# Rows repeated over partitions: TensorE selections and ScalarE copies replaced by DMAs inside SBUF, in a decoder step with a mixture of experts

## The chip, the cores and the metric

The kernel runs on one core of one Trainium2 chip. The metric is the device time of one execution in microseconds (us), median of several runs. A profile shows one execution: busy times and waits of TensorE (PE; PEld is its weight load), VectorE (DVE), ScalarE (ACT), GpSimd (POOL) and SyncE (SP), and what the DMA engines moved. SP computes nothing here; its program is a list of DMA issues and of semaphore waits, taken strictly in order. All its transfers go through one hardware queue (q1 in the profile).

## The reference, cut to what matters

One layer for 256 prompt tokens (one sequence) and 64 sample tokens (8 sequences of 8). Width 1024, everything in float32.

```
mod = silu(c) @ w_ada + b_ada                 # c: one row per sequence, 9 in all
sh1, sc1, gt1, sh2, sc2, gt2 = split(mod, 6)  # 1024 columns each
h = rmsnorm(x, g_mix) * (1 + sc1) + sh1
merged = sigmoid(ga) * (attention(h) @ w_pa) + sigmoid(gb) * (retention(h) @ w_pb)
x = x + gt1 * (merged @ w_o)
h2 = rmsnorm(x, g_ffn) * (1 + sc2) + sh2
x = x + gt2 * moe(h2)                         # top 4 of 32 experts, SwiGLU, 12.6 MB of weights each
y = rmsnorm(x, g_final)
```

The change is about sh2 (the "shift rows") and gt2 (the "gate rows"). Each is 9 rows of 1024: one for the prompt, 8 for the sample sequences. The mixture of experts needs them with tokens on partitions, so the prompt's row must stand on all 128 partitions (sh2p, gt2p), and each sample sequence's row on 8 of 64 partitions (sh2s, gt2s).

## The kernel before, in words

Each engine has a program written out by hand, and semaphores tie them together (wait_ge on one engine, then_inc on another). There is no scheduler: the order in the file is the order on the engine.

**Before the experts.** Weights come in 2 MB tiles. Tiles 17 to 25 hold, among others, the eight tiles of the modulation (w_mid), which modulation_step multiplies on TensorE between the branch projections. DVE's modulation_out(i) (line 2275) copies the sums of half i out of PSUM into mod_rows[i]: in half 0 stand gt1 and sh2, in half 1 sc2 and gt2. Partitions 64 to 72 and 96 to 104 of mod_rows hold the 9 rows of sh2 (or gt2), 512 columns in each group, and a small DMA puts the matching piece of b_ada on partition 73 and 105. modulation_transposes (line 1498) makes the column forms gt1T, sh2T, a2T from the same tile.

**Spreading the rows.** spread_rows(i) on TensorE (line 1509) multiplies 32 partitions of mod_rows[i] by the constant selp (ones on row 0 and on row 9, the bias), which adds the bias and repeats the prompt's row over 128 partitions, and by sels for the sample rows. ACT copies the results out of PSUM: sh2p and sh2s at lines 861 to 864, gt2p and gt2s at 874 to 877. spread_rows(0) runs right ahead of the output projection, spread_rows(1) (in final_gate_rows) after its third column tile.

**The output projection** is out_tile(c), c = 0 to 7 (line 1551): tile 26 of the weights serves c = 0 to 3, tile 27 the rest. Between the column tiles stand shift_logits (line 1575, sh2 times the router's weights wr, waits on rw_here, that is on the load of wr), spread_shift_logits (1582) and the router's product (1559). After each column tile DVE's x1_tile makes the new x, ACT squares it (869) and POOL adds the squares (680). Then come the norm, the router's logits and the top 4 on DVE (line 2345 to 2356; 2356 writes the selection), the position count on PE (1635, 1637), and h2 = normed x + shift: prompt tile 0 by DVE (2360), prompt tile 1 scaled by ACT (886) and shifted by POOL (683), the samples by DVE (2514). x_rows (1680) gathers the first expert's rows.

**The experts.** Weights come as 2 MB chunks, 6 to an expert, into 8 slots. gate_up_bias (line 1745) opens an expert; for the first one it waits on late_here, which counts the load of bgu (b_gate_up, line 541). gate_up (1759) takes chunks 0 to 3, down (1786) chunks 4 and 5. Chunk n is issued by SP once chunk n - 8 is used, so from here on the stream of chunks is tied to PE's progress. The first eight chunks are issued as their slots come free, during the output projection.

**SP's list around the change:** modulation tiles 21 to 23, the bias rows of half 0, b_router, tile 24, tiles 26 and 27 (w_out), wr, the bias rows of half 1, chunks 0 to 3 of expert 0, b_down, the final norm's row, chunk 4, one chunk of expert 1, chunk 5, bgu, another chunk of expert 1.

Of the kernel before, what the change touches and what calls it, by code (L numbers as in the profile page):

```python
# [16 lines left out]
ALU = mybir.AluOpType  # L17
# [55 lines left out]
def constants():  # L73
# [16 lines left out]
    t["selp"] = np.tile(((r % 32 == 0) | (r % 32 == 9))[:, None], (1, P))  # L90
    t["sels"] = ((r % 32)[:, None] == 1 + np.arange(NS)[None, :] // DS) | (r % 32 == 9)[:, None]
# [73 lines left out]
def kern(nc, a):  # L165
    with ExitStack() as ctx:
# [77 lines left out]
        mod_rows = [xr[:, 512 * i:512 * i + 512] for i in range(2)]  # L244

# [34 lines left out]
        def rt(at, n):  # L280
# [72 lines left out]
        h2s_done, rstd2_done, gT_tr, gT_done, ainit_mm, g2_mm, g2_done, late_here, flag_done = (sem(n) for n in (  # L353
            "h2s_done", "rstd2_done", "gT_tr", "gT_done", "ainit_mm", "g2_mm", "g2_done", "late_here", "flag_done"))
# [7 lines left out]
        yf_done, mul_done = sem("yf_done"), sem("mul_done")  # L362
        col_done, wo_mm, ut_done, pool_sum = sem("col_done"), sem("wo_mm"), sem("ut_done"), sem("pool_sum")
# [38 lines left out]
        def _(sp):  # L402
# [100 lines left out]
            load_modulation(20, 2)  # L503
            sp.wait_ge(sa_tr, PAIRS)
# [14 lines left out]
            load_bias_rows(1, g_here)  # L519
# [16 lines left out]
            sp.wait_ge(g2_mm, 2)  # L536
# [52 lines left out]
        def _(pool):  # L589
# [91 lines left out]
            pool.wait_ge(part_done, 5)  # L681
            pool.wait_ge(rows_done, 13)
            nc.gpsimd.tensor_tensor(h2[:, 1, :], h2[:, 1, :], sh2p, ALU.add).then_inc(pool_sum, 1)

        @block.scalar
        def _(act):
# [173 lines left out]
            act.wait_ge(tb_mm, 3)  # L860
            nc.scalar.activation(sh2p, bank(0, 2), ACT.Copy).then_inc(part_done, 1)
            act.wait_ge(tb_mm, 4)
            nc.scalar.activation(sh2s[0:NS, 0:BANK], bank(4)[0:NS], ACT.Copy)
            nc.scalar.activation(sh2s[0:NS, BANK:D], bank(4)[NS:P], ACT.Copy).then_inc(part_done, 1)
# [6 lines left out]
            for c in range(3):  # L871
                x1_square(c)
            act.wait_ge(g2_mm, 1)
            nc.scalar.activation(gt2p, bank(0, 2), ACT.Copy).then_inc(g2_done, 1)
            act.wait_ge(g2_mm, 2)
            nc.scalar.activation(gt2s[0:NS, 0:BANK], bank(4)[0:NS], ACT.Copy)
            nc.scalar.activation(gt2s[0:NS, BANK:D], bank(4)[NS:P], ACT.Copy).then_inc(g2_done, 1)
            for c in range(3, KT):
                x1_square(c)
# [20 lines left out]

            x1_rows_out(0)
# [109 lines left out]
        def _(pe):  # L1011
# [489 lines left out]
            def spread_rows(i, signal):  # L1501

                for name in ("selp", "sels"):
                    if i == 0 and name == "sels":
                        pe.wait_ge(rows_done, 12)
                    for k in range(2):
                        rows = slice(64 + 32 * k, 96 + 32 * k)
                        out = bank(4)[NS * k:NS * k + NS, :] if name == "sels" else bank(k)
                        last = nc.tensor.matmul(out, const(name)[rows], mod_rows[i][rows], start=True, stop=True)
                    last.then_inc(signal, 1)  # L1510

# [51 lines left out]
            def router_rows():  # L1563

                pe.wait_ge(part_done, 7)
# [20 lines left out]
            def final_gate_rows():  # L1586
                pe.wait_ge(g_here, 64)
                pe.wait_ge(part_done, 6)
                spread_rows(1, g2_mm)

            for c in range(KT):
# [5 lines left out]
                if c == 2:  # L1597
                    final_gate_rows()
# [21 lines left out]
            pe.wait_ge(g2_done, 2)  # L1620
# [261 lines left out]
        def _(dve):  # L1882
# [401 lines left out]
            for i in range(2):  # L2284
# [12 lines left out]
                if i == 0:  # L2297
                    dve.wait_ge(tb_mm, 1)
                    for half, (dst, at) in enumerate(((gt1T, 2 * KT), (sh2T, 3 * KT))):
                        nc.vector.tensor_tensor(by_chunk(dst), columns_of(half), spread(badaT[:, at:at + KT]),  # L2300
                                                ALU.add).then_inc(col_done, 1)
# [330 lines left out]
```

## Time and profile before

| | |
|---|---|
| runs, median (lowest to highest) | 1392.13 us (1390.81 to 1394.26) |
| the profiled execution, device time | 1390.95 us |
| its span in the profile | 1389.1 us |
| PE busy | 1353.6 us (97% of the span) |
| DVE, ACT, POOL busy | 501.1, 219.8, 67.6 us |
| moved by DMA | 487.81 MB, mean 351 GB/s |
| chain that ended last | PE 76%, DMA 18%, DVE 3%, ACT 1% |

PE is busy nearly all the time, and from about 486 us on the DMA engines move 425 to 430 GB/s without a break, so both are at work all through the experts. The experts' first matmul of gate_up stands at 455.0 us.

### The profile page before, as it was taken

The page shows a single profiled execution, that of the slowest core. Times are in us where ns is not written, and L with a number is a line of the kernel's source. Part 1 is how long each engine was busy: PE and PEld are TensorE (multiplying, and loading weights), DVE is VectorE, ACT ScalarE, POOL GpSimd, SP SyncE. Part 2 cuts the span into 40 slices and gives each one's busy share as a digit, 9 for nine tenths or more (in the row PEclk, how much of TensorE's full clock was granted, in tenths as well). Part 3 has the DMA queues.
Part 4 walks back from the last instruction along what each step waited for, and adds up shares of the span by engine and source line. Part 5 has one row for each costly group of instructions (what it writes and reads, how often), then busy time and mean ns, then how long its engine had stood idle before and what let it go on. Part 6 is the DMA issues. An engine that isn't in the chain of part 4 may idle for free.

```text
span 1389.1 us, 17563 instructions
## 1 busy us (share of the span) xinstructions
PE 1353.6 (97%) x6742; PEld 549.9 (40%) x6742; DVE 501.1 (36%) x1081; ACT 219.8 (16%) x407; POOL 67.6 (5%) x65
## 2 busy tenths in 40 slices
PE   8999999999999999999999999999999999999996
PEld 4544555555456333333333333333333333333332
DVE  3245887853124322332233222422223222233225
ACT  2111232121022211111111111111111111111102
POOL 1003402220001000000000000000000000000000
PEclk9999999999999999999999999999999999999998
DMA  9424354387877799999999999999999999999994
GB/s 387 161 98 166 122 128 159 105 311 272 345 314 307 280 428 428 428 426 428 428 430 427 428 428 430 428 428 427 430 428 428 427 430 429 427 428 429 430 425 185
DMA packets 62302, 487.81 MB, mean 351 GB/s; under 512 B 8327, under 2 KB 30407, under 8 KB 33836
## 3 DMA queue, kind: packets, MB, share of 16 engines
q1 hardware_dynamic: 59948, 482.43, 84.4%
q0 software_dynamic: 1152, 4.19, 0.8%
q8 instruction: 30, 0.49, 0.1%
q10 hardware_dynamic: 1152, 0.52, 0.1%
q14 instruction: 20, 0.16, 0.0%
HBM read 483.01 MB, written 4.08 MB: 351 GB/s over the span
## 4 chain that ended last, share of the span: by engine, by line
PE 76%; DMA 18%; DVE 3%; ACT 1%; issue 0%; SPq 0%; DVEq 0%
PE ps L1759 23%; PE ps L1786 12%; DMA z<-in_w_gate_up 10%; DMA ring<-in_w_gate_up 7%; PE ps L1068 6%; PE ps L1069 5%; PE ps L1680 5%; PE ps L1083 3%; PE ps L1731 3%; PE ps L1551 3%; PE ps L1745 2%; PE ps L1046 2%; PE ps L1735 1%; PE ps L1393 1%; PE ps L1382 1%; DMA ring<-in_w_mid 1%
## 5 line engine op out<-in xcount | busy, mean ns | idle before, releaser
L1759 PE MATMUL ps<-ring,z 128*64 128x512 f32 x1552 | 343.7, 594 | 9.8 <-DMA ring<-in_w_gate_up 9.1
L2455 DVE TENSOR_SCALAR actT<-ps 128x512 f32<-128x512 f32 x32 | 22.1, 692 | 589.6 <-PE ps L1759 589.6
L1759 PEld LDWEIGHTS ps<-ring,z 128*64 128x64 f32 x1552 | 108.5, 137 | 239.4 <-issue 217.6
L1786 PE MATMUL ps<-ring,z 128*64 128x512 f32 x752 | 167.7, 594 | 0.0
L1068 PE MATMUL ps<-ring,actT 128*128 128x512 f32 (+1 forms) x200 | 102.4, 594 | 1.3 <-DVE actT L1941 1.1
L1069 PE MATMUL ps<-ring,actT 128*128 128x512 f32 (+1 forms) x200 | 100.3, 583 | 0.0
L1786 PEld LDWEIGHTS ps<-ring,z 128*64 128x64 f32 x752 | 52.5, 137 | 109.9 <-issue 109.1
L1680 PE MATMUL ps<-z,actT 128*64 128x512 f32 x384 | 89.1, 597 | 0.2 <-DVE actT L2371 0.2
L1731 PE MATMUL ps<-z,aT 128*128 128x512 f32 x120 | 62.0, 619 | 0.0
L1759 PE MATMUL ps<-z 128*64 128x512 f32 x256 | 57.9, 594 | 3.0 <-DMA z<-in_w_gate_up 3.0
L2400 DVE TENSOR_TENSOR xr<-xr,z 128x512 f32<-128x512 f32 (+1 forms) x75 | 59.8, 797 | 2.6
L939 ACT ACTIVATE actT<-actT 128x512 f32<-128x512 f32 x30 | 18.8, 627 | 237.7 <-DVE actT L2455 237.7
L1069 PEld LDWEIGHTS ps<-ring,actT 128*128 128x128 f32 x200 | 38.0, 190 | 46.0 <-issue 45.0
L2392 DVE TENSOR_TENSOR z<-ps,z 128x512 f32<-128x512 f32 x60 | 41.4, 689 | 37.7 <-PE ps L1731 37.5
L1759 PE MATMUL ps<-more_w,z 128*64 128x512 f32 x240 | 54.5, 596 | 0.0
L924 ACT ACTIVATE z<-ps 64x512 f32<-64x512 f32 x30 | 17.7, 589 | 231.7 <-PE ps L1786 231.7
L1068 PEld LDWEIGHTS ps<-ring,actT 128*128 128x128 f32 x200 | 35.7, 190 | 42.2 <-issue 41.3
L1084 PE MATMUL ps<-ring,actT 128*64 128x256 f32 (+1 forms) x200 | 45.8, 379 | 0.0
L1083 PE MATMUL ps<-ring,actT 128*64 128x256 f32 (+1 forms) x200 | 45.8, 378 | 0.0
L2036 DVE MAX8 st<-ring 64x8 f32<-64x1032 f32 (+2 forms) x48 | 45.0, 937 | 1.3
L1680 PEld LDWEIGHTS ps<-z,actT 128*64 128x64 f32 x384 | 26.6, 137 | 46.3 <-issue 44.9
L2037 DVE MATCH_REPLACE8 ring<-st,ring 64x1032 f32<-64x1032 f32 (+2 forms) x48 | 44.1, 920 | 0.0
(370 smaller groups left out, 1305.1 us busy)
## 6 DMA issues: line engine op xcount, KB each, us to landing
ring<-in_w_gate_up SPq DMA_DIRECT2D x97, 2048.0 KB, 27.1
ring<-in_w_down SPq DMA_DIRECT2D x47, 2048.0 KB, 29.7
z<-in_w_gate_up SPq DMA_DIRECT2D x16, 2048.0 KB, 27.6
more_w<-in_w_gate_up SPq DMA_DIRECT2D x15, 2048.0 KB, 26.4
ring<-in_w_in SPq DMA_DIRECT2D x11, 2048.0 KB, 7.6
more_w<-in_w_down SPq DMA_DIRECT2D x9, 2048.0 KB, 30.6
ring<-in_w_mid SPq DMA_DIRECT2D x8, 2048.0 KB, 9.3
z<-in_w_down SPq DMA_DIRECT2D x8, 2048.0 KB, 33.0
```

The lines of the kernel that those rows point to most:

```text
L1068: nc.tensor.matmul(bank(b)[:, 0:w], hT[:, k, 0:P], w_z(i, k), **se)
L1069: last = nc.tensor.matmul(bank(b + 1)[:, 0:w], hT[:, k, P:2 * P], w_z(i, k), **se)
L1083: nc.tensor.matmul(bank(b)[0:NS, 0:h], hT[:, k, 2 * P:NTOK], w_z(i, k)[:, 0:h], **se)
L1084: last = nc.tensor.matmul(bank(b)[NS:P, 0:h], hT[:, k, 2 * P:NTOK], w_z(i, k)[:, h:w], **se)
L1551: last = nc.tensor.matmul(bank(6 + c % 2)[:, 0:NTOK], w[:, k, c % 4 * P:(c % 4 + 1) * P], hT[:, k, :], start=k == 0, stop=k == KT - 1)
L1680: last = nc.tensor.matmul(bank(3)[64 * i:64 * i + 64, :], S[:, t, :], h2[:, t, i * BANK:(i + 1) * BANK], start=t == 0, stop=t == 2)
L1731: nc.tensor.matmul(bank(b), SgT[:, t * P:(t + 1) * P], y[:, half * BANK:(half + 1) * BANK], start=True, stop=True).then_inc(cmb_mm, 1)
L1759: done = nc.tensor.matmul(bank(q // 2)[64 * (q % 2):64 * (q % 2) + 64, :], lhs, homes[home][4 * (k % 2) + q], start=False, stop=k == 7)
L1786: done = nc.tensor.matmul(bank(2)[64 * q:64 * q + 64, :], lhs, homes[home][2 * (k % 4) + q], start=k == 0, stop=k == 7)
L2036: step(nc.vector.max(m8, v))
L2037: step(nc.vector.match_replace(v, m8, v, TAKEN))
L2400: last = nc.vector.tensor_tensor(acc[0:n, t, c], acc[0:n, t, c], tmp3[t][0:n, c], ALU.add)
```

## The change

It does five things.

1. modulation_out(i) adds the bias on DVE, from bias_rows[i]: b_ada repeated over 9 partitions by DMA (four DMAs, issued early), in a region that POOL zeroes first (a memset of 128x1024).
2. spread_rows leaves TensorE (16 matmul instructions in all) and ACT (six copies). In its place SP issues, for each of sh2 and gt2, four DMAs from SBUF to SBUF: for each half of the columns one whose source is one row on one partition, read 128 times, and one whose source is 8 rows on 8 partitions, each read 8 times. That is 2 x 262,144 + 2 x 131,072 = 786,432 bytes written for each of the two.
3. Waits follow: DVE and POOL wait for sh2_here where they waited for ACT's copy; the wait for the last merged transposes (rows_done 12) moves into the middle of the first out_tile.
4. POOL's shift addition for prompt tile 1 is cut into four pieces of 256 columns.
5. The small DVE instruction that makes nmr moves from behind the selection to behind the first pick.

```
@@ constants: the bias row is no longer selected
-    t["selp"] = np.tile(((r % 32 == 0) | (r % 32 == 9))[:, None], (1, P))
+    t["selp"] = np.tile((r == 0)[:, None], (1, P))
@@ SP
             def load_bias_rows(i, signal):
-                sp.wait_ge(tb_mm, 1 + i)
                 for h in range(2):
                     at = (6 + 4 * i + h) * BANK
-                    sp.dma_start(mod_rows[i][73 + 32 * h:74 + 32 * h, :], a["b_ada"][:, at:at + BANK]).then_inc(signal, 16)
+                    sp.dma_start(bias_rows[i][64 + 32 * h:73 + 32 * h, :].unsqueeze(1),
+                                 a["b_ada"][:, at:at + BANK].partition_broadcast(1 + DB)).then_inc(signal, 16)
+
+            def spread_rows(i, prompt, sample, signal):
+
+                sp.wait_ge(partb_done, 1 + i)
+                for h in range(2):
+                    c = slice(BANK * h, BANK * (h + 1))
+                    rows = mod_rows[i][64 + 32 * h:73 + 32 * h, :]
+                    sp.dma_start(prompt[:, c], rows[0:1].unsqueeze(1).broadcast_to([1, P, BANK])).then_inc(signal, 16)
+                    sp.dma_start(sample[0:NS, c], rows[1:1 + DB].unsqueeze(1).broadcast_to([DB, DS, BANK])).then_inc(signal, 16)
...
             load_modulation(20, 2)
+            sp.wait_ge(z_zeroed, 3)
+            load_bias_rows(0, part_here)
+            load_bias_rows(1, g_here)
...
-            load_bias_rows(0, part_here)
             sp.dma_start(br, a["b_router"].partition_broadcast(P)).then_inc(rw_here, 16)
             load_modulation(24, 6)
+            sp.wait_ge(yb_mm, 1)
+            spread_rows(0, sh2p, sh2s, sh2_here)
             load_tile(26, in_tile("w_out", 0))
             load_tile(27, in_tile("w_out", 1))
             sp.wait_ge(tile_done, 26)
             sp.dma_start(wr, a["w_router"].rearrange("(k p) e -> p k e", p=P)).then_inc(rw_here, 16)
-            load_bias_rows(1, g_here)
+            spread_rows(1, gt2p, gt2s, gt2_here)
...
-            sp.wait_ge(g2_mm, 2)
+            sp.wait_ge(wo_mm, 3)
             chunk(1, 1, 7)
@@ POOL
+            nc.gpsimd.memset(xr[:, 1024:2048], 0.0).then_inc(z_zeroed, 1)
...
-            pool.wait_ge(part_done, 5)
+            pool.wait_ge(sh2_here, 16 * (DB + 4))
             pool.wait_ge(rows_done, 13)
-            nc.gpsimd.tensor_tensor(h2[:, 1, :], h2[:, 1, :], sh2p, ALU.add).then_inc(pool_sum, 1)
+            for c in range(4):
+                q = slice(256 * c, 256 * (c + 1))
+                last = nc.gpsimd.tensor_tensor(h2[:, 1, q], h2[:, 1, q], sh2p[:, q], ALU.add)
+            last.then_inc(pool_sum, 1)
@@ ACT: the copies into sh2p, sh2s, gt2p, gt2s are gone
+            act.wait_ge(sh2_here, 16 * (DB + 4))
+            act.wait_ge(gt2_here, 128)
             x1_rows_out(0)
@@ PE
-            pe.wait_ge(part_here, 48)
             pe.wait_ge(rows_done, 9)
-            spread_rows(0, tb_mm)
...
                 for k in range(KT):
+                    if c == 0 and k == KT // 2:
+                        pe.wait_ge(rows_done, 12)
@@ DVE
             def modulation_out(i):
                 dve.wait_ge(tile_done, 22 + 4 * i)
-                nc.vector.tensor_copy(mod_rows[i], bank(7 - i)).then_inc(partb_done, 1)
+                dve.wait_ge((part_here, g_here)[i], (48, 64)[i])
+                nc.vector.tensor_tensor(mod_rows[i], bank(7 - i), bias_rows[i], ALU.add).then_inc(partb_done, 1)
...
-            nc.vector.tensor_scalar(nmr, m8r[:, :, 0], -1.0, None, ALU.mult).then_inc(m0_done, 1)
-            dve.wait_ge(part_done, 5)
+            dve.wait_ge(sh2_here, 16 * (DB + 4))
...
             pick_bias(0, const("rowsel"), 0, True)
+            nc.vector.tensor_scalar(nmr, m8r[:, :, 0], -1.0, None, ALU.mult).then_inc(m0_done, 1)
```

SP's list of issues, from modulation tile 21 to the first chunks, before (xr holds mod_rows and, after the change, bias_rows; z holds the spread rows; ring, cT and aT hold weights):

```order
L428 DMA ring<-in_w_mid 128x4096 [waits tile_done] x3
L437 DMA xr<-in_b_ada 1x512 [waits tb_mm]
L437 DMA xr<-in_b_ada 1x512
L513 DMA aT<-in_b_router 128x32
L428 DMA ring<-in_w_mid 128x4096 [waits tile_done]
L428 DMA ring<-in_w_out 128x4096 [waits tile_done] x2
L518 DMA cT<-in_w_router 128x8x32 [waits tile_done]
L437 DMA xr<-in_b_ada 1x512 [waits tb_mm]
L437 DMA xr<-in_b_ada 1x512
L529 DMA ring<-in_w_gate_up 128x4096 x4
```

The same stretch of SP after the change:

```order
L430 DMA ring<-in_w_mid 128x4096 [waits tile_done]
L447 DMA z<-xr 128x1x512 [waits partb_done,yb_mm]
L448 DMA z<-xr 64x1x512
L447 DMA z<-xr 128x1x512
L448 DMA z<-xr 64x1x512
L430 DMA ring<-in_w_out 128x4096 [waits tile_done] x2
L533 DMA cT<-in_w_router 128x8x32 [waits tile_done]
L447 DMA z<-xr 128x1x512 [waits partb_done]
L448 DMA z<-xr 64x1x512
L447 DMA z<-xr 128x1x512
L448 DMA z<-xr 64x1x512
L544 DMA ring<-in_w_gate_up 128x4096 x4
```

Four copies inside SBUF now stand ahead of the two w_out tiles, and four more ahead of the first chunks of the experts.

PE from the last modulation transposes to shift_logits, before:

```order
L1498 MATMUL ps<-cst,xr 128x128 [waits col_done,partb_done]
L1498 MATMUL ps<-cst,xr 128x128 x3
L1509 MATMUL ps<-xr,cst 128x512 [waits rows_done,part_here]
L1509 MATMUL ps<-xr,cst 128x512
L1509 MATMUL ps<-xr,cst 64x512 [waits rows_done]
L1509 MATMUL ps<-xr,cst 64x512
L1551 MATMUL ps<-actT,ring 128x320 [waits w_here0]
L1551 MATMUL ps<-actT,ring 128x320 x7
L1575 MATMUL ps<-cT,mods 9x32 [waits rw_here,col_done]
```

The same stretch of PE after the change:

```order
L1507 MATMUL ps<-cst,xr 128x128 [waits col_done,partb_done]
L1507 MATMUL ps<-cst,xr 128x128 x3
L1549 MATMUL ps<-actT,ring 128x320 [waits w_here0,rows_done]
L1549 MATMUL ps<-actT,ring 128x320 x3
L1549 MATMUL ps<-actT,ring 128x320 [waits rows_done]
L1549 MATMUL ps<-actT,ring 128x320 x3
L1573 MATMUL ps<-cT,mods 9x32 [waits rw_here,col_done]
```

The four selections are gone, the first out_tile waits for w_here0 (the first w_out tile) right behind the transposes, and the wait for the last merged rows stands in its middle.

## Rows read from the trace of the kernel before

**Rows 1.** Chain of waits that ended last, in order of time: start us, us, what.

```profile
397.73 2.06 PE ps L1509 x8
399.79 4.50 PE ps L1551 x16
...
414.65 2.06 PE ps L1509 x8
...
445.78 1.70 issue
...
449.82 2.80 PE ps L1680 x12
```

**Rows 2.** Timeline of PE: start us, us, what, and idle time before.

```profile
399.72 4.57 PE L1551 MATMUL ps<-actT,ring 128*128 128x320 f32 x16
404.23 0.64 PE L1575 MATMUL ps<-cT,mods 128*9 128x32 f32 x16
...
452.55 1.09 PE L1745 MATMUL ps<-actT 32*64 32x512 f32 x8
...
455.00 13.95 PE L1759 MATMUL ps<-ring,z 128*64 128x512 f32 x64 [0.69 <-ACT z L915]
```

**Rows 3.** Timeline of SP's issues, same columns.

```profile
372.40 0.43 SPq L428 DMA_DIRECT2D ring<-in_w_mid  x1
383.57 10.83 SPq L428 DMA_DIRECT2D ring<-in_w_out  x2
395.79 0.38 SPq L518 DMA_DIRECT2D cT<-in_w_router  x1
397.76 0.54 SPq L437 DMA_DIRECT2D xr<-in_b_ada  x2
398.35 1.90 SPq L529 DMA_DIRECT2D ring<-in_w_gate_up  x4
```

**Rows 4.** Issues with KB and us to landing: w_out, wr, and the last store.

```profile
ring<-in_w_out SPq DMA_DIRECT2D x2, 2048.0 KB, 8.4
...
cT<-in_w_router SPq DMA_DIRECT2D x1, 128.0 KB, 7.9
...
y_sample<-z SPq DMA_DIRECT2D x1, 256.0 KB, 4.6
```

**Rows 5.** Stretches: us; busy (count) of PE, PEld, DVE, ACT, POOL; PEclk, DMA share, GB/s.

```profile
193.00:202.00 9.00, 9.00 (x28) 4.25 (x26) 8.79 (x11) 0.60 (x1) 0.00 (x0) 1.00 1.23 208
...
374.00:381.00 7.00, 7.00 (x17) 3.04 (x16) 0.00 (x0) 0.00 (x0) 0.00 (x0) 1.00 0.87 342
381.00:384.00 3.00, 3.00 (x20) 0.74 (x19) 0.00 (x0) 0.00 (x0) 0.00 (x0) 1.00 0.16 66
395.00:436.00 41.00, 41.00 (x187) 25.84 (x180) 10.38 (x41) 9.99 (x18) 4.29 (x5) 1.00 1.01 408
436.00:439.50 3.50, 3.50 (x16) 2.17 (x17) 0.59 (x3) 0.43 (x1) 0.86 (x1) 1.00 0.24 103
...
600.00:640.00 40.00, 40.00 (x188) 13.70 (x186) 7.41 (x14) 3.49 (x6) 0.00 (x0) 1.00 1.01 428
...
1376.70:1380.50 3.80, 0.00 (x0) 0.00 (x0) 3.50 (x6) 2.58 (x7) 0.00 (x0) 0.99 0.02 4
1380.50:1383.00 2.50, 0.00 (x0) 0.00 (x0) 2.29 (x7) 1.15 (x1) 0.00 (x0) 0.50 0.00 0
...
1386.20:1387.30 1.10, 0.00 (x0) 0.00 (x0) 0.00 (x0) 0.00 (x0) 0.00 (x0) 0.50 1.05 253
```

**Rows 6.** Timeline of POOL and DVE around the selection.

```profile
436.51 0.86 POOL L680 TENSOR_TENSOR z<-z 128x320 f32<-128x320 f32 x1 [3.45 <-ACT z L869]
445.14 2.35 POOL L683 TENSOR_TENSOR z<-z 128x1024 f32<-128x1024 f32 x1 [7.78 <-ACT z L886]
...
445.74 1.81 DVE L2356 TENSOR_SCALAR z<-z 128x96 f32<-128x96 f32 x1
...
449.10 0.58 DVE L2371 TENSOR_SCALAR actT<-cst,aT 128x64 f32<-128x64 f32 x3
```

More of the change, by code:

```diff
@@ L88, in constants @@
     r = np.arange(P)
-    t["selp"] = np.tile(((r % 32 == 0) | (r % 32 == 9))[:, None], (1, P))
-    t["sels"] = ((r % 32)[:, None] == 1 + np.arange(NS)[None, :] // DS) | (r % 32 == 9)[:, None]
+    t["selp"] = np.tile((r == 0)[:, None], (1, P))
+    t["sels"] = r[:, None] == 1 + np.arange(NS)[None, :] // DS
     i = np.arange(P)
@@ L244, in kern @@
         mod_rows = [xr[:, 512 * i:512 * i + 512] for i in range(2)]
+        bias_rows = [xr[:, 1024 + 512 * i:1536 + 512 * i] for i in range(2)]
         rqT = xr[:, 0:512].rearrange("p (c n) -> p c n", c=4)
@@ L352, in kern @@
             "lg_mm", "m0_done", "ex_done", "selm_done", "pos_mm", "gate_done"))
-        h2s_done, rstd2_done, gT_tr, gT_done, ainit_mm, g2_mm, g2_done, late_here, flag_done = (sem(n) for n in (
-            "h2s_done", "rstd2_done", "gT_tr", "gT_done", "ainit_mm", "g2_mm", "g2_done", "late_here", "flag_done"))
+        h2s_done, rstd2_done, gT_tr, gT_done, ainit_mm, g2_mm, late_here, flag_done = (sem(n) for n in (
+            "h2s_done", "rstd2_done", "gT_tr", "gT_done", "ainit_mm", "g2_mm", "late_here", "flag_done"))
         chunk_here = [sem(f"chunk_here{k}") for k in range(6)]
@@ L362, in kern @@
         yf_done, mul_done = sem("yf_done"), sem("mul_done")
+        sh2_here, gt2_here = vnew_here, dec_here
         col_done, wo_mm, ut_done, pool_sum = sem("col_done"), sem("wo_mm"), sem("ut_done"), sem("pool_sum")
@@ L859, in _ @@
                                          bank(3 * i + t)[:, 0:4 * n].rearrange("p (k n) -> p k n", k=4), ACT.Copy).then_inc(rows_done, 1)
[L860 to L864, printed above, removed]
             nc.scalar.activation(st[0:1, 38:39], st[0:1, 38:39], ACT.Sqrt)
@@ L869, in x1_square @@
                 nc.scalar.activation(sqc[c], x1c[c], ACT.Square).then_inc(ss2_done, 1)
[L871 to L878, printed above, removed]
+            for c in range(KT):
                 x1_square(c)
@@ L1499, in modulation_transposes @@
                 last.then_inc(tb_mm, 1)
[L1501 to L1510, printed above, removed]
             pe.wait_ge(side_here[0], 48)
@@ L1563, in router_rows @@
             def router_rows():
-                pe.wait_ge(part_done, 7)
+                pe.wait_ge(part_done, 5)
                 for t in range(3):
@@ L1619, in _ @@
             router_steps(4, KT - 1)
-            pe.wait_ge(g2_done, 2)
             pe.wait_ge(col_done, 5)
@@ L2298, in _ @@
                     dve.wait_ge(tb_mm, 1)
-                    for half, (dst, at) in enumerate(((gt1T, 2 * KT), (sh2T, 3 * KT))):
-                        nc.vector.tensor_tensor(by_chunk(dst), columns_of(half), spread(badaT[:, at:at + KT]),
-                                                ALU.add).then_inc(col_done, 1)
+                    nc.vector.tensor_tensor(by_chunk(gt1T), columns_of(0), spread(badaT[:, 2 * KT:3 * KT]), ALU.add).then_inc(col_done, 1)
+                    nc.vector.tensor_copy(by_chunk(sh2T), columns_of(1)).then_inc(col_done, 1)
             modulation_out(1)
@@ L2323, in _ @@
                 if c == 0:
-                    dve.wait_ge(tb_mm, 5)
+                    dve.wait_ge(tb_mm, 3)
                     nc.vector.tensor_copy(l2c[0:1 + DB], bank(2)[0:1 + DB, 0:NE]).then_inc(col_done, 1)
                 if c == 1:
-                    dve.wait_ge(tb_mm, 6)
+                    dve.wait_ge(tb_mm, 4)
                     dve.wait_ge(rw_here, 64)
@@ L2430, in start_result @@
                 if t == 0:
-                    dve.wait_ge(g2_done, 2)
+                    dve.wait_ge(gt2_here, 128)
                 tmp = tmp3[t][0:n, :]
@@ L2501, in experts @@
                 if base:
-                    dve.wait_ge(g2_mm, 3)
+                    dve.wait_ge(g2_mm, 1)
                 for t in range(3) if base else (1, 2):
@@ L2509, in _ @@
             pick_bias(0, const("rowsel"), 0, True)
+            nc.vector.tensor_scalar(nmr, m8r[:, :, 0], -1.0, None, ALU.mult).then_inc(m0_done, 1)
             dve.wait_ge(rows_tr, 15)
-            dve.wait_ge(part_done, 6)
             for i in range(2):
```

6 lines of the change are left out of this document (removed).

## The prediction

> **What bounds the kernel now.** I read the chain of waits first. From 397 to 450 us it runs through PE without a gap but one: the spreading of the shift rows, the column tiles of the output projection, the spreading of the gate rows, 1.70 us of waiting at 445.78, then the first expert's rows [rows 1]. So what PE drops there is on the path, unless another wait takes its place. PE's timeline gives the two marks that I use: the opening of the first expert (gate_up_bias) at 452.55 and its gate_up at 455.00 [rows 2]. From then on chunk n leaves only when chunk n - 8 is used, and the stretches show the queue at 428 GB/s [rows 5]. The stream of chunks is hung on those marks, so the end of the kernel moves by as much as they do.
>
> The second thing that bounds the stage is the one queue. It drains at about 381.5 us (the stretch from 381 to 384 moved 66 GB/s for 3 us, which is 0.2 MB), then takes the two w_out tiles issued from 383.57 on, and from 395 to 436 it is full at 408 GB/s; only from 436 to 439.5 does it run at a quarter (103 GB/s) [rows 3, 5]. Behind that stand bgu and one more chunk. The queue is therefore nearly as tight as PE, with some 3.5 us of air.
>
> **The change part by part.**
>
> *PE's selections.* Two groups of 2.06 us leave the path [rows 1]. The first is covered in part: shift_logits needs wr, issued at 395.79 and landed 7.9 us later, at 403.7 [rows 3, 4]. Before, it began at 404.23 [rows 2]; without the selections PE is there at 402.2 and waits to 403.8. That leaves 0.4 of 2.06. The second gives all of its 2.06. The wait moved into the first out_tile costs nothing: ACT's last merged copy was over when the selections' second half began, 1 us behind the first, and half an out_tile is 2.25 us.
>
> *POOL in four pieces.* DVE's writing of the selection took 1.81 us, though it is 96 columns wide; it began at 445.74, POOL's shift addition at 445.14, and both ended at 447.5 [rows 6]. So it stood behind POOL's instruction. In pieces of 256 columns POOL takes 0.86 + (2.35 - 0.86) x (256 - 320) / 704 = 0.72 us each, about 2.9 us in all. The selection is then let in after the first piece, 1.4 us earlier, but the pick at 449.10, an instruction of the same kind, meets the later end of POOL. I take 0.8 us, bounds 0 and 1.4. The Trainium skill (SBUF — State Buffer, "Who interferes with whom") says that such a DVE instruction and a GpSimd one take the shared port pair in turn, for the whole instruction; these rows agree.
>
> *DVE, ACT, small DMAs.* modulation_out is one DVE instruction as before, from PSUM, with the same 512 columns. The bias loads and POOL's memset stand early, in the attention of the samples, where SP's list waits for PE anyway. ACT's six copies were off the path. All of these I put at nothing; if the memset held up a DVE copy there, it would be 1 us.
>
> *The eight copies inside SBUF.* This decides. Each group writes 0.786 MB, of which 0.524 MB are read from one row on one partition per copy, and 0.262 MB from eight rows on eight partitions. At the queue's 428 GB/s a group takes T = 1.8 us. But the stretches show that a transfer which reaches fewer partitions is slower: the loads of the retention state, into 64 partitions, ran at 208 GB/s from 193 to 202 us with the DMA engines busy throughout, and the last store, from 64 partitions, at 253 [rows 5, 4], against 428 for all 128. Half the partitions, about half the rate. Nothing in the trace reads one partition at length. If the rate went on falling with the number of partitions, one partition would give 428 / 128 = 3.3 GB/s and a group would take 160 us. That is the far bound; the near one is 1.8. Between ends so far apart I go by what halving suggests, a limit per group of partitions and not per partition: 16 DMA engines share 428, so one share is 26.8 GB/s. The 0.524 MB then take 19.6 us, and the sample rows, spread over eight partitions, between 0.6 and 9.8; I take 3. **T = 22.5 us per group**, an estimate from rows of another shape.
>
> The Trainium skill has a rule for this (SBUF — State Buffer, "Door 1: The DMA port swizzle"): SBUF has 16 DMA ports of 27.2 GB/s, and partitions 64 to 67 and 96 to 99 share one. By it both prompt rows and three of eight sample rows are read through one port, 0.622 MB or an estimated 22.9 us a group. The rows on 64 partitions agree with it; no run here yet shows one partition.
>
> *The sum.* The queue runs in order. The shift copies start at 381.5 and end at 404.0. The first w_out tile (2.10 MB, 4.9 us) lands at about 409.9, with 1 us from last byte to signal. PE wanted it at 397.7: 12 us of waiting there. Next come the second w_out tile (4.9), wr (0.8), the gate copies (22.5), four chunks (19.6), b_down and the norm's row (0.9), three chunks (14.7) and bgu (0.6 + 1.0). So bgu lands at 381.5 + 2T + 47.4 = 428.9 + 2T = **473.9 us**. PE, held up first by the w_out tile, would be at gate_up_bias at 409.9 + (452.55 - 399.72) - 2.06 - 0.8 + 1.2 (for wr) = 461.1 and waits there for 12.8 us. The mark moves from 452.55 to 473.9, by 21.3 us. On the profiled execution's own 1390.95 us that is 1412.3; the median of the runs lies 1.2 above that execution, so **1413 us**. What PE saves is swallowed by the two waits.
>
> Chunks 0 to 3 have landed by then (457), so gate_up follows as before.
>
> **The rivals.**
>
> *The copies are quick and hidden* (the other side: not slower). If T is 1.8 us, the shift copies end at 383.3, before the first w_out tile is issued, and the gate copies only use up air: bgu lands at about 443, wanted at 449. Then the sum is -0.4 - 2.06 - 0.8 = -3.3 us: 1388.8. If wr landed early enough to free the whole first group, it would be -4.9, or 1387.2. It decides from T under 10. For it: the store from 64 partitions kept 253 GB/s, above half. Against it: both rows on 64 partitions. Chance 0.32.
>
> *A middle rate.* The sum comes out at zero where 428.9 + 2T = 452.55, so at T = 11.8, which is 67 GB/s. T from 10 to 14 gives 1389 to 1397. It would take a source of one partition with a third of the rate of 64. Chance 0.10.
>
> *Worse than one share.* If one partition gives half a share, T is about 42 and the mark moves by 60 us: 1452. A smaller extra: PE's granted clock fell from 0.99 to 0.50, from 2.4 to 1.2 GHz, once it had stood still from 1376.7 to 1380.5 [rows 5]. A wait of 12 us would do that here too, and some of the bias and the first matmuls would run at the lower level: 1 to 4 us more. Chance of over 1421: 0.08.
>
> **How the numbers follow.** Forecast 0.50; quick copies 0.32, of which 0.12 go beyond 0.3% (under 1388, 4.2 us, about what a measurement of this kernel can tell from no change) and 0.20 stay within; middle rate 0.10, of which 0.07 within and 0.03 slower; worse 0.08. Faster 0.12, within 0.3% 0.27, slower 0.61. The forecast's own range, from a T of 19 (the prompt rows alone) to 25, is 1406 to 1420. Cases of both signs hold most of the chance, so the range reaches from 1388 to 1421 and leaves out the worst and the best.
>
> **What the profile of the changed kernel would show.** Right: between 381 and 404 and again before the first chunks, stretches in which the DMA engines are busy and move some 30 GB/s; PE idle ahead of the first out_tile with a w_out DMA as releaser; gate_up_bias near 474, waiting for bgu. The selection on DVE under 0.6 us, with POOL in four pieces of 0.7. Wrong: the copies land within 3 us of their issue, PE goes from the transposes to out_tile without a gap, and shift_logits waits for wr to about 403.8. The forecast falls if a single source partition gives more than 67 GB/s, or if later tiles in the queue overtake the copies on idle DMA engines.

## The result, and the profile after

Slower. The kernel after takes 1417.09 us (1415.2 to 1417.46, 4 runs), the kernel before 1391.7 us (1390.81 to 1394.26, 4 runs beside them): a ratio of 1.018, 95% interval 1.0166 to 1.0192, so 25.4 us more. The forecast was 21 us more. The profiled execution took 1416.86 us, 25.9 more than the one before. Below, the mark is the start of gate_up_bias, and bgu is the load of b_gate_up that it waits for.

PE's timeline of the kernel after, columns as in [rows 2]. L1549 is out_tile, L1573 the shift logits, L1735 gate_up_bias, L1749 gate_up.

```profile
400.01 0.66 PE L1507 MATMUL ps<-cst,xr 128*128 128x128 f32 x4
411.04 7.39 PE L1549 MATMUL ps<-actT,ring 128*128 128x320 f32 x16 [10.37 <-DMA ring<-in_w_out]
418.36 0.64 PE L1573 MATMUL ps<-cT,mods 128*9 128x32 f32 x16
...
460.45 2.79 PE L1670 MATMUL ps<-z,actT 128*64 128x512 f32 x12 [0.23 <-DVE actT L2360]
475.36 1.98 PE L1735 MATMUL ps<-actT 32*64 32x512 f32 x8 [12.11 <-DMA actT<-in_b_gate_up]
...
479.08 16.90 PE L1749 MATMUL ps<-ring,z 128*64 128x512 f32 x64 [0.69 <-ACT z L924]
```

Both waits of the forecast are there: 10.4 us for w_out, 12.1 us for bgu. gate_up_bias begins at 475.36, not at 452.55 [rows 2]: 22.8 us later. Behind each wait something more was lost. The first out_tile takes 7.39 us and the first gate_up 16.90, where they took 4.57 and 13.95 [rows 2].

The stretches say why, and what the queue did. Columns as in [rows 5].

```profile
386.00:397.00 11.00, 11.00 (x78) 5.50 (x76) 3.23 (x6) 1.36 (x3) 0.00 (x0) 1.00 0.92 35
...
399.00:411.00 12.00, 1.67 (x15) 1.19 (x13) 0.89 (x3) 2.85 (x5) 0.00 (x0) 0.67 0.93 339
...
416.00:431.00 15.00, 15.00 (x71) 10.44 (x70) 4.36 (x19) 1.41 (x3) 1.57 (x2) 0.97 0.88 33
...
403.50:416.50 13.00, 5.46 (x10) 3.54 (x11) 0.00 (x0) 0.00 (x0) 0.00 (x0) 0.50 0.85 237
468.00:485.00 17.00, 8.96 (x26) 2.75 (x28) 0.00 (x0) 1.88 (x2) 0.00 (x0) 0.50 0.54 226
```

Twice, from 386 to 397 and from 416 to 431, the DMA engines are busy nine tenths of the time and move 33 to 35 GB/s: a busy share alone would say that the queue works at full rate. These are the two groups of copies. And in both waits PE's granted clock fell to 0.50, that is 1.2 of 2.4 GHz, and it was still there for some microseconds after PE had begun again.

SP's own timeline shows a second face of the gate copies, which [rows 3] has no like of:

```profile
403.41 8.72 SPq L447 DMA_DIRECT2D z<-xr  x1
...
412.92 7.15 SPq L447 DMA_DIRECT2D z<-xr  x1
420.11 9.91 SPq L448 DMA_DIRECT2D z<-xr  x1
430.06 7.50 SPq L544 DMA_DIRECT2D ring<-in_w_gate_up  x4
...
451.22 0.33 SPq L556 DMA_DIRECT2D actT<-in_b_gate_up  x1
```

L447 and L448 are the copies. An issue that took 0.5 to 0.7 us for the shift group now takes up to 9.9: SP itself stands still while the engines are behind, and the first expert's chunks, issued at 398.35 before [rows 3], leave at 430.06.

The small gain came too. POOL and DVE around the selection, to be read against [rows 6]:

```profile
457.01 2.78 POOL L701 TENSOR_TENSOR z<-z 128x256 f32<-128x256 f32 x4 [7.77 <-ACT z L893]
...
457.62 0.21 DVE L2346 TENSOR_SCALAR z<-z 128x96 f32<-128x96 f32 x1
...
459.72 0.58 DVE L2360 TENSOR_SCALAR actT<-cst,aT 128x64 f32<-128x64 f32 x3
```

The selection takes 0.21 us in place of 1.81, and the pick (L2360) begins at 459.72, before the last piece ends. In this kernel the gain is swallowed by the wait for bgu; what it is worth alone is measured in experiment 5.

One thing I had not looked for: PE was 2.9 us behind before the first wait (L1507 ends at 400.67; the part after it began at 397.73 [rows 1]). It comes from about 306 us. There the copy of the transposed probabilities out of PSUM (L2228), due when PE let it go at 305.66, started late, PE waited 1.71 us for it, and the clock fell to 0.50 for some 3 us, from 311 to 314. Timeline and stretches of the kernel after:

```profile
306.24 0.94 POOL L666 DMA_INDIRECT ring<-in_cache_v,irow  x1 [0.30 <-issue]
...
307.17 0.97 POOL L690 MEMSET xr<- 128x1024 f32 x1
...
308.33 1.23 DVE L2228 COPY ring<-ps 128x1024 f32<-128x1024 f32 x1 [5.29 <-remote]
```

```profile
310.00:312.00 2.00, 2.00 (x32) 1.98 (x30) 1.39 (x2) 0.23 (x1) 0.00 (x0) 0.74 1.06 392
312.00:314.00 2.00, 2.00 (x15) 1.35 (x13) 0.28 (x1) 0.98 (x2) 0.00 (x0) 0.50 1.05 372
```

The change's memset ran right there, so my first theory was the memset.

### The profile page after: what moved, and what is told of

Same layout as the page of the kernel before. It is cut to its first block, busy times and chain, and to the rows that moved or that the text cites. A ratio compares the mean times of both kernels' runs of the same rounds, so it can differ in the third digit from the quotient of the medians.

```text
span 1415.2 us, 17538 instructions
## 1 busy us (share of the span) xinstructions
PE 1358.8 (96%) x6726; PEld 553.1 (39%) x6726; DVE 499.4 (35%) x1081; ACT 215.4 (15%) x401; POOL 68.9 (5%) x69
## 4 chain that ended last, share of the span: by engine, by line
PE 76%; DMA 19%; DVE 3%; ACT 1%; another core or an unknown queue 0%; issue 0%; SPq 0%; DVEq 0%
PE ps L1749 24%; PE ps L1776 13%; DMA z<-in_w_gate_up 7%; DMA ring<-in_w_gate_up 7%; PE ps L1077 5%; PE ps L1078 5%; PE ps L1670 5%; PE ps L1721 3%; PE ps L1092 3%; PE ps L1549 3%; PE ps L1735 2%; DMA ring<-in_w_out 2%; DMA actT<-in_b_gate_up 2%; PE ps L1055 1%; PE ps L1725 1%; PE ps L1402 1%
## 5 line engine op out<-in xcount | busy, mean ns | idle before, releaser
L1749 PE MATMUL ps<-ring,z 128*64 128x512 f32 x1552 | 346.6, 598 | 9.5 <-DMA ring<-in_w_gate_up 8.8
L1749 PEld LDWEIGHTS ps<-ring,z 128*64 128x64 f32 x1552 | 109.1, 138 | 241.6 <-issue 220.0
L1749 PE MATMUL ps<-z 128*64 128x512 f32 x256 | 57.8, 593 | 2.8 <-DMA z<-in_w_gate_up 2.8
L948 ACT ACTIVATE actT<-actT 128x512 f32<-128x512 f32 x30 | 18.8, 627 | 240.3 <-DVE actT L2444 240.3
L1749 PE MATMUL ps<-more_w,z 128*64 128x512 f32 x240 | 54.5, 596 | 0.0
L1549 PE MATMUL ps<-actT,ring 128*128 128x320 f32 x128 | 38.3, 461 | 10.4 <-DMA ring<-in_w_out 10.4
L1735 PE MATMUL ps<-actT 32*64 32x512 f32 x256 | 35.7, 627 | 12.1 <-DMA actT<-in_b_gate_up 12.1
```

Of the source, the lines that this page charges most:

```text
L1735: nc.tensor.matmul(bank(q // 2)[64 * (q % 2):64 * (q % 2) + 64, :], ebuf[32 * q:32 * q + 32], bgu[32 * q:32 * q + 32], start=True, stop=False)
L1749: done = nc.tensor.matmul(bank(q // 2)[64 * (q % 2):64 * (q % 2) + 64, :], lhs, homes[home][4 * (k % 2) + q], start=False, stop=k == 7)
```

## The experiments

### 1. The copies by themselves

A program of its own. VectorE fills the sources, then SP issues one DMA after another, each awaited:

```
def rep(name, p0, n, total=P):
    return s[name][p0:p0 + n, :].unsqueeze(1).broadcast_to([n, total // n, BANK])
...
one((dst[:, :], rep("s8", 64, 8)))
one((dst[:, :], rep("s4", 64, 4)))
one((dst[:, :], rep("s2", 64, 2)))
one((dst[:, :], rep("s1", 64, 1)))
one((dst[:, :], rep("s1z", 0, 1)))
```

> A program of its own, without the reference's computation: DMAs inside SBUF, one at a time, each awaited before the next, all to 128 partitions x 2 KB (256 KB), with the source on 128, 64, 32, 16, 8, 4, 2 and 1 partitions (read over and over), then 8 partitions to 64 (128 KB), two one-partition copies together from neighbouring and from distant partitions, and last the same 256 KB read from one row of DRAM and from 128 rows of DRAM. Theory, one partition is what is slow: the 256 KB take about 7.3 us (35 GB/s) from one partition, and the time falls as partitions are added, to under 2.5 us at 8 and above; two copies from partitions 64 and 65 take about 14.6 us if the limit is one of a neighbourhood, 7.3 us if it is one of a partition, and from 32 and 96 about 7.3 us. Rival, any copy inside SBUF is slow, whatever its source: all of them take 7 us or more, the one from 128 partitions too. Second rival, reading one row over and over is slow wherever it lies: the DRAM row takes 7 us as well.

One stretch of each copy; last two columns DMA share and GB/s. In this order: source on 64, 32, 16, 8, 4, 2 partitions, on partition 64 alone, on partition 0 alone, two copies together from 64 and 65, two from 32 and 96.

```profile
12.00:14.00 2.00, 0.00 (x0) 0.00 (x0) 1.00 0.60 131
15.00:18.00 3.00, 0.00 (x0) 0.00 (x0) 1.00 0.48 87
19.00:22.00 3.00, 0.00 (x0) 0.00 (x0) 1.00 0.75 87
24.00:28.00 4.00, 0.00 (x0) 0.00 (x0) 1.00 0.46 50
31.00:40.00 9.00, 0.00 (x0) 0.00 (x0) 1.00 0.23 25
43.00:52.00 9.00, 0.00 (x0) 0.00 (x0) 1.00 0.12 25
55.00:63.00 8.00, 0.00 (x0) 0.00 (x0) 1.00 0.92 28
67.00:74.00 7.00, 0.00 (x0) 0.00 (x0) 1.00 0.90 27
82.00:99.00 17.00, 0.00 (x0) 0.00 (x0) 1.00 0.90 27
103.00:118.00 15.00, 0.00 (x0) 0.00 (x0) 1.00 0.85 30
```

One, two and four neighbouring partitions all give 25 to 28 GB/s, eight give 50. (The first three rows hold the start or the end of a short copy and understate it; inside its copy, from 20 to 21 us, the source on sixteen partitions gave 98.) The DMA share tells that the number of busy engines is not the limit: two partitions kept two engines' worth busy (0.12), one kept nearly all sixteen (0.92), at about the same rate. This agrees with the Trainium skill (SBUF — State Buffer, "Door 1: The DMA port swizzle"), by which four neighbouring partitions share one port of 27.2 GB/s.

SP's issues give the time of one awaited copy, as the distance to the next issue:

```profile
64.70 0.52 SPq L190 DMA_DIRECT2D dst<-s1z  x1
75.82 0.69 SPq L190 DMA_DIRECT2D dst<-s8r  x1
80.12 0.48 SPq L190 DMA_DIRECT2D dst<-sa  x1
...
100.85 0.47 SPq L190 DMA_DIRECT2D dst<-sc  x1
...
119.67 0.39 SPq L190 DMA_DIRECT2D dst<-in_b_ada  x1
123.00 0.34 SPq L190 DMA_DIRECT2D dst<-in_w_mid  x1
125.63 44.94 SPq L190 DMA_DIRECT2D dst<-s  x8
```

256 KB from one partition: 11.1 us. 128 KB from eight partitions (the sample rows): 4.3 us. 256 KB from one row of DRAM: 3.3 us, from 128 rows of DRAM 2.6. The eight copies ahead of these, which the view merges into one row a turn, give by their issues one by one 2.4 us from 128 partitions, then 3.0, 3.6, 4.4, 6.9, 12.1, 12.2 and 11.2 us from 64, 32, 16, 8, 4, 2 and 1 partition. Both rivals fall: neither copies inside SBUF nor repeated rows are slow as such. So repeating a row costs little; repeating it out of one SBUF partition, or out of a few neighbours, does. The one-partition copy missed my 7.3 us, which I had worked out from the 35 GB/s of a whole group, and the sources on 8 to 64 partitions missed my "under 2.5 us". Two one-partition copies in one queue take 20.7 us from 64 and 65 and 18.8 from 32 and 96: the second waits behind the first even where it reads far away (one microsecond, from 111 to 112, moved 78 GB/s where the two meet; the rest ran at some 30). The 7.3 us for distant ones fell.

### 2. Both prompt sources wide, and one of them

```
-sp.dma_start(prompt[:, c], rows[0:1].unsqueeze(1).broadcast_to([1, P, BANK]))
+sp.dma_start(prompt[:, c], mod_rows[i][:, :])
```

> The changed kernel with the four prompt copies read from all 128 partitions, in place of one row repeated: same destinations, bytes and places in the queue, other values in the prompt's shift and gate. Theory, the one source partition makes the stalls: no wait for w_out at the first output tile, none for b_gate_up, no clock fall behind them; what stays is the two removed row spreads (2 x 2.06 us), the GpSimd pieces (1.2 us) and the 3.0 us lost early: 1391.7 - 4.1 - 1.2 + 3.0 = 1389.4 us (1388 to 1392). Rival, copies inside SBUF at this place in the queue are slow or in the way whatever they read: 1410 us or more.

Measured: 1387.35 us against 1389.8 for before on the same chip, a ratio of 0.998 (0.9971 to 0.999). PE's timeline has no wait for w_out and none for bgu:

```profile
396.98 4.47 PE L1549 MATMUL ps<-actT,ring 128*128 128x320 f32 x16
403.26 0.63 PE L1573 MATMUL ps<-cT,mods 128*9 128x32 f32 x16 [1.81 <-DMA cT<-in_w_router]
...
448.07 1.09 PE L1735 MATMUL ps<-actT 32*64 32x512 f32 x8
```

Same copies, same bytes, same places in the queue: only the source rows differ, and the whole loss is gone. (The prompt's shift and gate then hold other values; which instructions run doesn't hang on them.) That the copies stand in the queue costs nothing that shows. The 1.81 us for w_router is close to the 1.6 us that were foreseen when the first spread goes: it gives 0.25 of its 2.06 us. The early 2.9 us were absent in this execution, with the memset in its place.

> The changed kernel with only the two prompt shift copies read from all 128 partitions; the gate copies are as in the changed kernel. Theory, the groups add up in one queue (each delays all behind it by its own 14 to 21 us): w_out is in time, b_gate_up lands about 450 to 455 us, where TensorE comes at about 450, so it waits 0 to 5 us: 1390 to 1397 us. Rival, the wait at b_gate_up comes from the gate copies alone: it stays at 12 us with its 3 us of clock loss, and the time is 1391.7 - 5.3 + 3.0 + 15 = 1404 us.

Measured: 1402.44 us, a ratio of 1.0087 (1.007 to 1.0103). The rival was right. With only the gate copies slow, the wait at bgu is nearly whole:

```profile
398.26 3.17 SPq L447 DMA_DIRECT2D z<-xr  x1
401.47 13.55 SPq L448 DMA_DIRECT2D z<-xr  x1
```

```profile
461.09 1.98 PE L1735 MATMUL ps<-actT 32*64 32x512 f32 x8 [11.23 <-DMA actT<-in_b_gate_up]
...
464.82 15.92 PE L1749 MATMUL ps<-ring,z 128*64 128x512 f32 x64 [0.69 <-ACT z L924]
```

The gate copies can't leave before PE has reached tile 26, and the second w_out tile not before a slot is free, so the queue has air ahead of them whatever the shift group does (from 391 to 394 it moved 33 GB/s here, at a DMA share of 0.08). The formula 428.9 + 2T counts a queue that is full from 381.5 on, which needs a long shift group. With a quick one the gate group starts at about 400.5; the queue is slow until about 420, so T is some 20 us, and bgu lands at 461, about 440 + T. That 440 is fitted to this one run; by the terms of the prediction it would be 437.

### 3. The shift copies behind the w_out tiles

On the late zeroing (next), whose expectation it names:

```
+load_tile(26, in_tile("w_out", 0))
+load_tile(27, in_tile("w_out", 1))
 spread_rows(0, sh2p, sh2s, sh2_here)
-load_tile(26, in_tile("w_out", 0))
-load_tile(27, in_tile("w_out", 1))
```

> The kernel with the late zeroing (1.016 times the time of before), with one more edit: the four shift copies are issued behind the two w_out tiles instead of ahead of them. Theory, what sets the first expert's start is the sum of all that the one queue has to carry: w_out is in time, the wait of 9 us and its clock fall are gone, but the copies still stand ahead of the chunks, the wait at b_gate_up grows to 22 us or more, and the time stays within 3 us of the late zeroing's: 1.014 to 1.018 times before. Rival, the two waits are separate and each can be had back by order alone: 9 to 12 us faster, 1.007 to 1.009.

Measured: 1428.42 us, a ratio of 1.0257 (1.0241 to 1.0272). Neither. w_out is in time, but I had overlooked what stands behind the copies now: w_router, which the shift logits need. PE's timeline, and the stretch over both groups:

```profile
432.97 1.01 PE L1574 MATMUL ps<-cT,mods 128*9 128x32 f32 x16 [29.30 <-DMA cT<-in_w_router]
...
486.34 1.98 PE L1736 MATMUL ps<-actT 32*64 32x512 f32 x8 [6.66 <-DMA actT<-in_b_gate_up]
```

```profile
403.00:442.00 39.00, 9.70 (x46) 6.59 (x45) 3.13 (x14) 0.94 (x2) 0.56 (x1) 0.61 0.84 37
```

Two groups one behind the other held the queue for 39 us, about 20 a group. This order doesn't hide that; it only picks who waits.

### 4. The zeroing later

```
+pool.wait_ge(so_done, PAIRS)
 nc.gpsimd.memset(xr[:, 1024:2048], 0.0).then_inc(z_zeroed, 1)
```

> The changed kernel with GpSimd's zeroing of the 128 x 1024 block moved from 307 us to behind the last sample output (about 347 us), where VectorE is idle for 10 us, and the four bias rows' loads moved behind the loads of x. Theory, the zeroing holds up VectorE's copy at 306 us, and TensorE's wait with the clock fall behind it costs 3.0 us: 1417.1 - 3.0 = 1414.1 us, and VectorE's copy starts right when TensorE releases it. Rival, the 3 us come from something else in that stretch (the gathers, the queue): 1417 us and the late start stays.

Measured: 1412.62 us, a ratio of 1.0158 (1.0141 to 1.0174), where the theory's 1414.1 would be 1.0161; and in the profiled execution VectorE's copy did start with its release. Taken alone this speaks for the memset. To have the kernel after beside such ratios on another chip, it ran once more:

> The changed kernel itself once more, to have it on one chip with the others. If the early 3.0 us depend on a chance meeting of GpSimd's gathers and zeroing with VectorE's copy, its executions fall in two groups 2 to 3 us apart, and the profiled one shows the copy's late start or not; its median stands 1.018 times before, 2 to 3 us over that of the late zeroing where most executions meet. Rival, the hold-up is always there: one narrow group 3 us over it.

Measured: 1415.4 us where before took 1392.02, a ratio of 1.0164 (1.015 to 1.0178), one spread from 1414.49 to 1416.85 and not two groups. The two ratios don't differ measurably. That the memset is not needed for the late start is settled by a kernel that has none there, the next one: its copy starts late all the same. So it does in shift_behind (307.35) and in bounce (308.18), which both have the memset at its later place.

The late zeroing has another use: in its profiled execution nothing is lost at 306 us, so its waits can be held against the forecast's own numbers. PE's timeline:

```profile
407.50 6.43 PE L1550 MATMUL ps<-actT,ring 128*128 128x320 f32 x16 [9.14 <-DMA ring<-in_w_out]
...
471.64 1.98 PE L1736 MATMUL ps<-actT 32*64 32x512 f32 x8 [12.89 <-DMA actT<-in_b_gate_up]
```

### 5. The pieces alone

```
+for c in range(4):
+    q = slice(256 * c, 256 * (c + 1))
+    last = nc.gpsimd.tensor_tensor(h2[:, 1, q], h2[:, 1, q], sh2p[:, q], ALU.add)
```

on the kernel before, with the nmr instruction moved as in the change.

> The kernel before, with only GpSimd's shift addition in four pieces and the small VectorE instruction (nmr) moved as in the change; no copies, the spreads stay on TensorE. Theory, VectorE's selection waits for the shared port for one piece instead of the whole addition: 1.0 to 1.3 us faster, a ratio of 0.9992; the selection shrinks from 1.81 to under 0.6 us. Rival, the later end of the pieces holds up the pick behind it and nothing is won: 1.0000, with the pick late instead.

Measured: 1390.76 us against 1392.02, a ratio of 0.9992 (0.9983 to 1.0001): the size foreseen, though the interval just reaches no change. The selection takes 0.21 us. And at 306 us, without any memset:

```profile
305.79 0.94 POOL L651 DMA_INDIRECT ring<-in_cache_v,irow  x1 [0.30 <-issue]
...
307.86 1.23 DVE L2241 COPY ring<-ps 128x1024 f32<-128x1024 f32 x1 [5.02 <-remote]
...
309.32 0.29 PE L1430 MATMUL ps<-ring,z 128*64 128x8 f32 x4 [1.43 <-DVE ring L2242]
```

The copy starts 2.07 us after the last gather's start. In the kernel after it is 308.33 - 306.24 = 2.09, with a memset between. So the second theory is that GpSimd's gathers hold it. The view itself puts the late release down to "remote", which names none of this core's engines; the two semaphores that the copy waits for are counted up by PE alone.

### 6. The rows by way of DRAM

What is slow is one SBUF partition as source, and a row of DRAM is not. So the nine rows of a group are stored in y_prompt, which the result overwrites at the end, and read back from there (on the late zeroing):

```
+sp.dma_start(a["y_prompt"][16 * i:16 * i + 9, BANK * h:BANK * (h + 1)],
+             mod_rows[i][64 + 32 * h:73 + 32 * h, :]).then_inc(bounced, 16)
...
+rows = a["y_prompt"][16 * i:16 * i + 9, c]
+sp.dma_start(prompt[:, c], rows[0:1].partition_broadcast(P)).then_inc(signal, 16)
```

> The kernel with the late zeroing, with the slow reads replaced: the nine rows of each group are first stored in DRAM (in the first rows of y_prompt, which the result overwrites at the end), and the prompt and sample copies are read from there, repeated. The shift rows are stored before the w_out tiles are issued and read after them. Theory, only the one-partition source was slow; the DRAM row took the micro program under 1.5 us for 256 KB. No wait at w_out or b_gate_up, no clock fall, and all of the other savings are kept: 2.06 of the second spread, 0.4 of the first (w_router lands at 403), 1.2 of the pieces: 3.7 us under before, a ratio of 0.9973 (0.996 to 0.999). Rival, repeated reads of one row of DRAM are slow too beside the weights, or the wait for the stored rows holds up the queue: above 1.000.

Measured: 1394.43 us, a ratio of 1.0018 (1.0009 to 1.0027). So the expected gain did not come. The waits at w_out and bgu are gone, but the reads of the shift rows and the stores of the gate rows now stand ahead of w_router: SP issues it at 400.06, as PE ends its transposes, where in before it did so 1.9 us ahead of that point, and it takes 8.8 us to land in place of 7.9. PE waits for it, and the clock falls in the wait:

```profile
409.00 1.01 PE L1584 MATMUL ps<-cT,mods 128*9 128x32 f32 x16 [4.63 <-DMA cT<-in_w_router]
```

```profile
407.00:414.00 7.00, 5.00 (x24) 3.56 (x25) 0.18 (x1) 0.00 (x0) 0.00 (x0) 0.52 0.64 156
```

In another order (against bounce):

```
 store_rows(0)
+spread_rows(0, sh2p, sh2s, sh2_here)
 load_tile(26, in_tile("w_out", 0))
 load_tile(27, in_tile("w_out", 1))
-spread_rows(0, sh2p, sh2s, sh2_here)
-store_rows(1)
 sp.wait_ge(tile_done, 26)
 sp.dma_start(wr, ...)
-spread_rows(1, gt2p, gt2s, gt2_here)
+store_rows(1)
...
 chunk(0, k, k)
+spread_rows(1, gt2p, gt2s, gt2_here)
```

> The rows by way of DRAM as in bounce, in another order: the shift rows are read back ahead of the w_out tiles, where the queue stood empty for 2 to 3 us; w_router goes ahead of the storing of the gate rows, and these are read back behind the first four chunks. Theory, what bounce lost was w_router alone (4.6 us of waiting at the shift logits and the half clock from 407 to 414 us behind it): the wait shrinks to 1.8 us as with the wide sources, the clock stays up, and the ratio goes from 1.0018 to 0.9975 (0.9965 to 0.9985). Rival, reading a row of DRAM repeatedly costs the queue enough to make a new wait, at w_out or at b_gate_up: above 1.000.

Measured: 1390.09 us against 1391.54, a ratio of 0.9987 (0.9978 to 0.9996). PE's wait for w_router is 0.84 us in the profiled execution. Faster than before, by less than expected (0.9965 to 0.9985); that execution still shows the late copy at 307.41.

### 7. The gathers out of the copy's way

```
 if b in (4, 6):
     pool.wait_ge(st_out[b // 2 - 2], 64)
+if b == 6:
+    pool.wait_ge(so_done, 1)
```

> bounce_order with one more wait: GpSimd issues the gathers of samples 6 and 7 only when VectorE has written the first pair's output (about 311 us), where it is idle for 3 us. Theory, a VectorE copy that is released while GpSimd works on a gather is held until 2.05 us after the last gather's start; with the gathers out of its way it starts 0.1 us after its release in every execution, and where the other kernels show the hold-up this one is 1.4 to 2.5 us faster: 0.9960 to 0.9968. Rival, the copy's late start has nothing to do with gathers: it shows here too, and the ratio is that of bounce_order.

> The kernel before with GpSimd's shift addition in four pieces (0.9992 when run alone) and the two gathers put off as in bounce_gap. Same theory: where before shows the hold-up, 1.4 to 2.5 us faster than the pieces alone, 0.9975 to 0.9982; the copy starts 0.1 us after its release. Rival: 0.9992 and the late start stays.

Measured: bounce_gap 1387.26 us, a ratio of 0.9971 (0.9959 to 0.9983); pieces_gap, which has no copies at all, 1388.54 us, 0.9978 (0.9969 to 0.9987). In both the copy starts within 0.1 us of its release. (Four of the ten other profiled executions show that too, so two executions alone would prove little.) The timeline of pieces_gap:

```profile
305.44 1.23 DVE L2243 COPY ring<-ps 128x1024 f32<-128x1024 f32 x1 [2.66 <-PE ps L1449]
...
311.60 0.94 POOL L651 DMA_INDIRECT ring<-in_cache_v,irow  x1 [7.32 <-DVE ring L2253]
```

pieces_gap lies 0.0014 under the pieces alone and bounce_gap 0.0016 under bounce_order: 2 us each time, from moving two gathers, though the intervals of each pair overlap a little. The executions of pieces_gap also lie close together, 1388.12 to 1389.46, where those of the pieces alone ran from 1389.87 to 1394.08. Two microseconds are nearly what the whole change wins where its copies are quick (2.5 in wide_both, the pieces' 1.3 among them). bounce_gap stays just outside the 0.9960 to 0.9968 that I expected. Its profiled execution, a slow one of its range (1390.95 of 1385.44 to 1393.76), waits 1.95 us for w_router, and the clock falls behind that; the out_tile after it takes 6.27 us and not 4.57.

## Why the prediction came out right

**The rate of a single partition.** Right, by the reading of 64 partitions at 208 GB/s against 428 for all: the limit goes by groups of partitions. Foreseen 26.8 GB/s, measured 27 to 28 alone and 33 to 35 in a group whose sample rows come from more partitions. The divisor, 16, was reached by counting DMA engines, and experiment 1 shows that it is not their number that limits. Of the two rows on 64 partitions only the one at 208 GB/s gives half the rate; the last store's 253 lies above it.

**T = 22.5 us per group.** Right for the gate group, wrong for the shift group. In the kernel after, the queue is slow from 412.5 to 434, which is 21.5 us; in wide_shift it is some 20, in shift_behind about 20 each. But the shift group slows it from 384.5 to 399 only: 14.5 us.

**w_out at 409.9.** It landed at 411.0, but by other terms. The copies began 3.0 us late, since all was 3 us late; full rate was back 8.0 us sooner than T says; and then the first tile took 12 us and not 5.9: from 399 to 411 the queue moved 339 GB/s x 12 us = 4.1 MB, both tiles. The errors cancel to 1.1 us. They may belong together: the first tile was whole only with the second, as it would be if a part of the queue was still at the slow rows while the rest had gone on to the tiles. No view shows that part by itself, so this is argued. PE's wait was 10.4 us, foreseen 12.

**bgu at 473.9, a wait of 12.8.** It was 475.4 and 12.1. The mark moved by 22.8, foreseen 21.3, and this is closer than it deserves: the late copy's 2.9 us are in that, and the prediction had no such term. In late_zero, which lost nothing at 306 us, w_out lands at 407.5 and bgu at 471.6, each some 2.3 us sooner than foreseen, and the mark moves by 19.1.

**The clock.** Named as an extra of 1 to 4 us and left out of the sum: the term that was mis-sized, at nothing in place of 3.8. gate_up_bias and gate_up took 0.89 + 2.95 = 3.8 us longer. The first wait's loss, 2.8 us in out_tile, cost nothing, since PE then waited for bgu anyway. The mark's 22.8 and these 3.8 make 26.6; the profiled executions lie 25.9 apart and the medians 25.4. What won back the last microsecond stays open.

**The selections and the pieces.** The second spread gave its 2.06, the first 0.25 (0.4 foreseen). The pieces: from the second group of square sums (453.34) to the first expert's rows (460.45) PE takes 7.11 us, against 8.35 before; alone, 1392.02 - 1390.76 = 1.3 us (0.8 foreseen, bounds 0 to 1.4).

**The memset at nothing.** Right as far as two ratios that don't differ can tell (late_zero and after_again), and my own later doubt of it was not borne out. What did cost something in that stretch, the late copy, the prediction didn't have.

**The rivals' prices.** Quick copies: wide_both is that case, 2.5 us under before, where 3.3 was worked out. The middle rate: its formula, 428.9 + 2T, does not hold where the shift group is short; wide_shift's landing fits 440 + T. Both reach 452.55 at nearly the same T (11.8 and 12.5), so that rival's place would have stood. My expectation for wide_shift, which added the groups up in the same way, was 9 us too early for bgu (452 against 461).

**A slip.** The upper end of the forecast's range, 1420 for a T of 25, comes to 1418.5 by the prediction's own formula (428.9 + 50 = 478.9, 26.35 us behind 452.55). The result lies inside either.

## What to carry to other kernels

A row that is to be repeated over partitions should not be read by DMA out of one SBUF partition, nor out of a few neighbours: here it held a queue of 428 GB/s at some 30 GB/s, and all weights behind it. Let TensorE spread it, or store it to DRAM and read it back repeated (0.9987 of the time before, against 1.0164 for the change as it stands), with those reads placed where the queue has air and behind nothing that somebody waits for. Before moving a transfer ahead or back in a queue, list each load behind it with its own deadline; the smallest one (w_router, 128 KB) decided two of these runs.

## What the runs showed of the hardware

A copy out of PSUM by VectorE was held back while GpSimd worked through its gathers. In the profiled executions of six kernels it began 2.0 to 2.1 us after the start of the last gather (after 2.09, before_pieces 2.07, bounce_order 2.08, shift_behind 2.06, after_again 2.03, bounce 2.01), and 2.0 to 2.7 us after PE had released it, with a memset behind the gather or without. In before, wide_both, wide_shift and late_zero it began within 0.1 us of its release, though the same four gathers ran around it, a few tenths of a microsecond shifted. Putting two gathers off removed the hold-up in both kernels tried. What in a gather holds the copy, and what decides between the two cases, stays open.

PE's granted clock fell to half, to 1.2 GHz, in the waits of 10.4 and 12.1 us in the kernel after, 11.2 in wide_shift and 4.6 in bounce. After short waits it fell in some executions and not in others, and always only after PE had begun again. At 308 us it fell behind 1.71 us in the kernel after and behind 1.35 in after_again (a mean of 0.62 from 309 to 313), and not behind 1.73 in bounce nor 1.43 in before_pieces (1.00 there). At w_router it fell behind 1.88 us in wide_shift (0.50 from 404.0 to 407.2) and 1.95 in bounce_gap (0.50 from 409 to 411), and not behind 1.81 in wide_both (1.00 from 401 to 406). So the length of such a wait doesn't tell. Each fall at w_router made the next out_tile 1.7 us longer (6.26 and 6.27 in place of 4.57), nearly as much again as the wait. The half clock outlasted the long waits: to 416.5 after one that ended at 411.0, to 485 after one that ended at 475.4.

The DMA busy share is no measure of a queue's work: 0.92 at 28 GB/s from one partition, 0.12 at 25 GB/s from two.
